# Running sums of the second attention's softplus: two reduced-precision parts instead of one full-precision operand

## What is computed

```python
z = einsum('bqkgd,bskd->bkgqs', qb, kf)              # logits
log_1m_beta = where(mask, log_sigmoid(-z), 0.0)      # minus the softplus of z, strictly causal
rev = cumsum(log_1m_beta, axis=4, reverse=True)
excl = concatenate([rev[..., 1:], zeros], axis=-1)
a = where(mask, exp(log_sigmoid(z) + excl), 0.0)
o = einsum('bkgqs,bskd->bqkgd', a, vf)
```

## The kernel before, in words

| step of | before |
|---|---|
| TensorE | sums 5, 7, 8, 12; values 8, 10, 12, 14 |
| ScalarE | shares 3, 5, 6, 10; logarithm 4, 6, 6, 10; weights 7, 9, 9, 13; out_high 9, 10, 13, 15 |
| VectorE | masked 2, 4, 6, 10; softplus 4, 6, 7, 10; less 6, 7, 8, 12; out_low 8, 10, 13, 15 |

## Time and profile before

### The profile page before, as it was taken

How to read it: one execution, slowest core, us unless ns; L and a number is a source line. 1 busy time by engine, 2 the same in 40 slices (tenths; PEclk the granted TensorE clock), 3 DMA queues, 4 the chain that set the end, 5 groups by cost and what they waited for, 6 DMA issues and landing times.

```text
span 2041.1 us, 30539 instructions
## 1 busy us (share of the span) xinstructions
PE 1908.4 (93%) x12761; PEld 1485.7 (73%) x12761; DVE 1136.2 (56%) x1523; ACT 903.7 (44%) x1289; POOL 113.3 (6%) x99
## 2 busy tenths in 40 slices
PE   9999999999999866766799999999999999999998
PEld 7898988889983211111178888888888888988887
DVE  3788877678542110101156666756666766766666
ACT  4655555554342100000045556545446555676544
POOL 0333331001000000000000000000000000000000
PEclk9999999999999977887899999999999999999999
DMA  9645447778799999999985755555555555525552
GB/s 349 214 149 170 160 158 230 233 260 288 281 367 415 425 427 425 425 426 424 421 292 196 242 189 183 171 165 170 191 191 171 186 187 188 178 93 176 186 186 83
DMA packets 241777, 503.51 MB, mean 247 GB/s; under 512 B 11473, under 2 KB 165730, under 8 KB 222434
## 3 DMA queue, kind: packets, MB, share of 16 engines
q1 hardware_dynamic: 241024, 500.96, 68.2%
q10 hardware_dynamic: 610, 0.53, 0.1%
HBM read 500.07 MB, written 1.07 MB: 246 GB/s over the span
## 4 chain that ended last, share of the span: by engine, by line
PE 80%; DMA 12%; DVE 4%; issue 2%; ACT 2%; SPq 1%; POOL 0%; DVEq 0%; ACTq 0%
PE bank L651 15%; PE bank L653 15%; PE bank L652 15%; PE bank L712 14%; PE bank L714 7%; DMA m<-in_expert_w_down 4%; DMA m<-in_expert_w_up 4%; PE bank L1115 3%; DMA m<-in_expert_w_gate 3%; PE bank L1126 2%; PE bank L996 1%; DVE m L2314 1%; SPq L3430 1%; PE bank L1390 1%; PE bank L810 0%
## 5 line engine op out<-in xcount | busy, mean ns | idle before, releaser
L2314 DVE TENSOR_TENSOR m<-m,m 128x1024 fp32r<-128x1024 f32 x505 | 626.7, 1255 | 282.7 <-ACT m L1599 281.5
L651 PE MATMUL bank<-m,m 128*128 128x256 f32 (+1 forms) x1960 | 657.9, 336 | 2.7 <-DVE m L2314 1.1
L653 PE MATMUL bank<-m,m 128*128 128x256 f32 (+1 forms) x1960 | 645.6, 329 | 0.0
L652 PE MATMUL bank<-m,m 128*128 128x256 f32 (+1 forms) x1960 | 645.3, 329 | 0.0
L1599 ACT ACTIVATE m<-m 128x1024 fp32r<-128x1024 f32 x505 | 524.7, 1054 | 212.2 <-PE bank L653 196.5
L712 PE MATMUL bank<-m,m 128*128 128x512 f32 x1248 | 439.8, 394 | 0.0
L651 PEld LDWEIGHTS bank<-m,m 128*128 128x128 f32 x1960 | 368.5, 188 | 49.8 <-issue 9.2
L653 PEld LDWEIGHTS bank<-m,m 128*128 128x128 f32 x1960 | 368.5, 188 | 36.7
L652 PEld LDWEIGHTS bank<-m,m 128*128 128x128 f32 x1960 | 368.8, 188 | 34.1 <-issue 1.2
L714 PE MATMUL bank<-m,m 128*128 128x256 f32 x1248 | 352.7, 283 | 0.0
L712 PEld LDWEIGHTS bank<-m,m 128*128 128x128 f32 x1248 | 234.4, 188 | 54.0
(11 more groups left out here) (353 smaller groups left out, 1377.9 us busy)
## 6 DMA issues: line engine op xcount, KB each, us to landing
m<-in_ffn_w_in SPq DMA_DIRECT2D x88, 1024.0 KB, 5.1
m<-in_w_in SPq DMA_DIRECT2D x60, 1024.0 KB, 5.2
m<-in_ffn_w_out SPq DMA_DIRECT2D x44, 1024.0 KB, 4.9
m<-in_expert_w_up SPq DMA_DIRECT2D x40, 1024.0 KB, 20.9
m<-in_expert_w_down SPq DMA_DIRECT2D x34, 1024.0 KB, 17.1
m<-in_expert_w_gate SPq DMA_DIRECT2D x33, 1024.0 KB, 22.9
m<-in_expert_w_gate SPq DMA_DIRECT2D x15, 2048.0 KB, 23.5
m<-in_expert_w_down SPq DMA_DIRECT2D x13, 2048.0 KB, 17.8
```

The costliest lines, as they stand in the source:

```text
L651: e.matmul(o, s[0], m[0], start=first, stop=False, skip_group_check=skip)
L652: e.matmul(o, s[0], m[1], start=False, stop=False, skip_group_check=skip)
L653: return e.matmul(o, s[1], m[0], start=False, stop=last, skip_group_check=skip)
L2314: inc(e.tensor_tensor(rv(fit(q.L, q.view.shape)), q.view, fit(q.H, q.view.shape), ALU.subtract), "l", skey(q, "L"))
```

## The change

The softplus of each group is split once more: GpSimd copies each half of t_ into fp32r at the place of l_ (the high part), and VectorE subtracts it from t_ in place (the low part). `sums` then makes, for each of three banks, two matmuls of 512 columns with SLI and two with ONES that cover 128 columns (banks 0 and 2) or two separate tiles of 128 (bank 1), all in fp32r. SLI and ONES are stored as fp32r. The steps are placed anew:

| step of | after |
|---|---|
| TensorE | sums 6, 8, 11, 13 (at 13 behind values(2)); values 8, 10, 13, 14 |
| ScalarE | shares 3, 5, 6, 10; logarithm 4, 6, 9, 10; weights 7, 8, 12, 14; out_high 9, 10, 13, 15 |
| VectorE | masked 2, 4, 6, 10; softplus 4, 6, 10, 12; low_part 5, 6, 10, 12; less 6, 8, 12, 13; out_low 9, 10, 13, 15 |

```diff
                 def sums(j, first):
                     b = [take(first + i, "sc", j, i) for i in range(3)]
-                    sp = sbuf[j][1]
-                    for n in range(12):
-                        w.wait_ge("ssp", j, n // 6)
-                        o = b[n // 4][:, 128 * (n % 4):128 * (n % 4) + 128]
-                        ins = e.matmul(o, SLI, sp[:, 128 * n:128 * n + 128], start=True, stop=n % 3 != 1, skip_group_check=True)
-                        if n % 3 == 1:
-                            ins = e.matmul(o, K(C_ONE), sp[:, 128 * n + 128:128 * n + 256], start=False, stop=True,
-                                           skip_group_check=True)
-                        if n % 4 == 3:
-                            full(ins, "sc", j, n // 4)
+                    H, L = spHL[j]
+                    for i in range(3):
+                        o = slice(512 * i, 512 * i + 512)
+                        w.wait_ge("spL", j, (512 * i + 511) // 768)
+                        e.matmul(b[i][:, :], SLI, H[:, o], start=True, stop=False, skip_group_check=True)
+                        e.matmul(b[i][:, :], SLI, L[:, o], start=False, stop=False, skip_group_check=True)
+                        if i == 1:
+                            w.wait_ge("spL", j, 1)
+                            out = b[1][:, :].rearrange("p (g n) -> p g n", n=128)[:, 0:4:3]
+                            m = [z.rearrange("p (g n) -> p g n", n=128)[:, 5:9:3] for z in (H, L)]
+                        else:
+                            c = 128 if i == 0 else 256
+                            out = b[i][:, c:c + 128]
+                            m = [z[:, 512 * i + c + 128:512 * i + c + 256] for z in (H, L)]
+                        e.matmul(out, ONES, m[0], start=False, stop=False, skip_group_check=True)
+                        full(e.matmul(out, ONES, m[1], start=False, stop=True, skip_group_check=True), "sc", j, i)
...
                 for step in range(15):
-                    if step in (5, 7, 8, 12):
-                        j = (5, 7, 8, 12).index(step)
-                        sums(j, 4 if j > 1 else 0)
-                    if step in (8, 10, 12, 14):
-                        values(step // 2 - 4)
+                    if step in (6, 8, 11):
+                        j = (6, 8, 11).index(step)
+                        sums(j, 4 if j else 0)
+                    if step in (8, 10, 13, 14):
+                        values((8, 10, 13, 14).index(step))
+                    if step == 13:
+                        sums(3, 4)
...
+                def low_part(j):
+                    l_, t_, z_ = sbuf[j]
+                    for q in range(2):
+                        o = slice(768 * q, 768 * q + 768)
+                        w.wait_ge("spH", j, q)
+                        H, L = spHL[j]
+                        inc(e.tensor_tensor(L[:, o], t_[:, o], H.bitcast(F32)[:, o], ALU.subtract), "sb", ("spL", j, q))
...
+            e.tensor_copy(ONES, K(C_ONE))
...
+            for j in range(4):
+                l_, t_, z_ = sbuf[j]
+                for q in range(2):
+                    o = slice(768 * q, 768 * q + 768)
+                    w.wait_ge("ssp", j, q)
+                    inc(e.tensor_copy(spHL[j][0][:, o], t_[:, o]), "att", ("spH", j, q))
```

More of the change, by code:

```diff
@@ L558, in build @@
         kk_of = [[kk[64 * i:64 * i + 64].rearrange("p (b h n) -> p h b n", b=2, h=2)[:, h] for h in range(2)] for i in range(2)]
-        gone, SLI = mem(20736, 768), mem(22016, 128)
+        gone, SLI, ONES = mem(20736, 768), rv(mem(22016, 128)), rv(mem(55232, 128))
         osT = hl(39456, 41504, 2048)
@@ L562, in build @@
         sbuf = [[mem(o, 1536) for o in so_[3 * j:3 * j + 3]] for j in range(4)]
+        spHL = [[rv(mem(o, 1536)) for o in so_[3 * j:3 * j + 2]] for j in range(4)]
         z_at = [0]
@@ L2044, in stick @@
                         shares(2)
-                        logarithm(2)
                     if step == 7:
                         weights(0)
+                    if step == 8:
+                        weights(1)
                     if step == 9:
                         out_high(0)
-                        weights(1)
-                        weights(2)
+                        logarithm(2)
                     if step == 10:
@@ L2056, in stick @@
                         logarithm(3)
+                    if step == 12:
+                        weights(2)
                     if step == 13:
                         out_high(2)
+                    if step == 14:
                         weights(3)
@@ L3028, in stick @@
                         masked((2, 4, 6, 10).index(step))
[L3029 to L3032, removed]
+                    if step == 4:
+                        softplus(0)
+                    if step == 5:
+                        low_part(0)
+                    if step == 6:
+                        softplus(1)
+                        low_part(1)
+                        less(0)
                     if step == 8:
-                        less(2)
+                        less(1)
+                    if step == 9:
                         out_low(0)
                     if step == 10:
+                        softplus(2)
                         out_low(1)
+                        low_part(2)
+                    if step == 12:
+                        less(2)
                         softplus(3)
-                    if step == 12:
+                        low_part(3)
+                    if step == 13:
+                        out_low(2)
                         less(3)
-                    if step in (13, 15):
-                        out_low(step // 2 - 4)
+                    if step == 15:
+                        out_low(3)
                     yield
```

## The result

The changed kernel takes 2046.7 us, median of 16 runs (2045.79 to 2049.74), against 2043.32 for 16 runs of the kernel before (2042.34 to 2045.49): ratio 1.0018, 95% interval 1.0011 to 1.0025. That is 3.4 us slower; the forecast was 2048.0 with a range of 2043 to 2055. The profiled execution was 2049.39 us with a span of 2047.6.

A forecast was written before the change was run, and what follows sets the result against it. TensorE's own work was taken as the bound. Minus 5.6 (sums) and 1.6 (old waits), plus about 9.9 (new waits) and 2.0 (clock) gave about 4.7 us slower: 2048.0 us median, range 2043 to 2055.

The forecast's parts named there:

- saved in the sums: TensorE's sums: a group falls from 3.5 to 2.1 us, saving 5.6 us in all (bounds 6.5 and 3.8).
- old waits gone: TensorE's two earlier waits for sums, 1.2 and 0.4 us, disappear: 1.6 us saved.
- first wait, logits(2): TensorE, half a piece into piece 6, idles 1.0 us before logits(2) for q2's evacuation.
- second wait, piece 10: TensorE idles 5.0 us before piece 10, which needs group 0's output, out_low(0); the largest term.
- third wait, values(2): TensorE idles 3.1 us before values(2), until ScalarE has made weights(2).
- net of all but the clock: Through the end of values(3), the new order costs 2.7 us net, sums' saving included.
- clock, first fall: After the wait before piece 10, TensorE's granted clock falls and costs 1.7 us.
- clock, second fall: After the wait before values(2), a fall adds 0.3 us, mostly hidden since sums(3) waits for VectorE anyway.
- copy, low_part: Added work: a GpSimd copy of 768 columns into fp32r takes 1.3 us, a VectorE subtraction 0.95 us.
- Waits without a fall: Rival: TensorE's new waits come but its clock stays up; plus 2.7, 2046.0 us; chance 0.20.
- TensorE stays the only bound: Rival: weights(0) to out_low(0) takes under 6 us, so piece 10 does not wait; 2037.1 us; chance 0.10.
- GpSimd's copies: Rival: copies bound the softplus-to-less line of groups 1 and 3, from about 1.8 us each; 2052 to 2058; chance 0.20.

The follow-up runs named there:

- e7: Changed kernel plus 16 idle f32 matmuls of 128 columns on TensorE before the first bo piece: 2045.06 us (before 2043.84).
- e5: The changed kernel measured again, its steps written out singly, as base for four further runs: 2048.32 us (before 2043.84).
- e4: The step order of e3, but with the f32 sums of the kernel before: 2043.23 us (before 2043.52).
- e3: Changed kernel's fp32r format in another step order, with out_high(0) ahead of weights(1) and less(0) ahead of softplus(1): 2037.81 us (before 2043.52).
- e1: Changed kernel's step order with the f32 sums of the kernel before, no split or GpSimd copies: 2045.51 us (before 2043.52).
- e8: Changed kernel with each GpSimd copy done twice: 2054.45 us (before 2043.84).
- e6: Changed kernel with ScalarE's weights(1) moved from step 8 to step 9, behind out_high(0): 2044.17 us (before 2043.84).
- e9: Changed kernel without VectorE's low_part; sums multiply the high part twice and wait for the copies alone: 2047.1 us (before 2043.84).

## Why the prediction was right, and where it was off

The sign, the mechanism and the places were right, and the total was 4.7 against 4.16 us in the stage (3.4 by medians of 16 runs). The single waits missed by 0.5 to 1.0 us and the total by only 0.5: where TensorE comes later to a gate, the wait is shorter and the gate stays where it is. By its own steps:

| step | forecast | measured |
|---|---|---|
| saved in the sums | 5.6 (1.4 a group) | 6.1 (1.5 a group) |
| old waits gone | 1.6 | 1.6 |
| first wait, logits(2) | 1.0 | 1.46 |
| second wait, piece 10 | 5.0 | 4.05 |
| third wait, values(2) | 3.1 | 2.15 |
| waits at values(0), sums(2) | 0.4, 0.2 | 0, 0 |
| waits at sums(3), piece 14, values(3) | 0.6, 0.5, 0.6 | 1.0, 0.2, 0.2 (e7); 0, 0, 0.19 (changed) |
| net of all but the clock | +2.7 | +2.0 (e7 against before) |
| clock, first fall | 1.7 | 2.1 (e5 against e7) |
| clock, second fall | 0.3 | 0 |
| copy, low_part | 1.3, 0.95 | 1.28, 1.1 |

- *The sums* were forecast from the 0.11 us row of the first attention; the pair of 128 columns takes 0.17, so one is 0.085. The range for it, half to double, held this. One group was read for all four: in e4 they take 3.5 to 3.6 us and in e3 2.0 to 2.1, 5.9 us less in all, and another 0.2 lie around them.
- *The first wait* was 0.5 too short in the forecast, because the walk took L of that piece at 1.2 us. It ran beside the first copies and took 1.85, so q2's evacuation came at 1790.33. In e1, with no copies, the wait is 0.83.
- *The second wait* was the term mis-sized most: out_low(0) ended 0.4 us earlier than walked and TensorE came 0.5 later, the other side of the first wait. In the walk's own time (minus 2.37) TensorE started piece 10 at 1810.6 against 1811.0. The chain of ten links was right to 0.4 us; the wait, a difference of two walks, was off by twice that.
- *The third wait*: in the walk's time, and without the 2.1 us of the clock, values(2) started at 1830.4 (1834.92 less 4.5) against 1831.1, and TensorE came to it at 1828.3 instead of 1828.0. Again two small errors of opposite sign add up in the wait.
- *The clock.* By the earlier trace rows 1.7 us was read from the expert stage, where TensorE at half speed worked for part of 5 us. Here 2.1 were lost: the clock was 0.50 from about 1811.0 to 1817.9, twice as long as in the expert stage of the kernel before (910.4 to 913.8), and for the first 1.9 us of it TensorE still waited. The second fall came, against my doubt, and cost nothing on balance, as I had argued: from values(2) to piece 14 the changed kernel takes 5.20 us at the low clock (1834.92 to 1840.12), and e7 takes 5.19 at full clock (1829.53 to 1834.72), since it waits 1.0 us for low_part(3) and 0.2 for out_low(2) instead. The Trainium skill, "TensorE: Matmul & The Clock Gate", section "HAM oscillation", says that an idle gap halves the clock; both falls of the changed kernel agree; the gaps of 1.46 us and e7's gap of 2.15 us had none.
- *The rivals.* "Waits without a fall" is e7: 2045.06, forecast 2046.0. "TensorE stays the only bound" was forecast at 2037.1 and is what e3 reaches at 2037.81, with another order. Its condition, a line from weights(0) to out_low(0) under 6 us, was wrong: the line takes 9.5 us there, and less(1) still stands ahead of out_low(0). What the third order did was to move weights(1) behind out_high(0) and to begin the line 4.7 us earlier. "GpSimd's copies" shows as waits for low_part before the sums at twice their price (e8); from which price on was not measured.

The balance of the stage: -6.1 for the sums, -1.6 for the old waits, +7.85 for the new ones, +2.2 for the first fall (7.2 against 5.0 us for piece 10 with logits(3)), +1.6 for the second (5.20 us from values(2) to piece 14 against 3.63 in e3; it takes the place of e7's waits at sums(3) and piece 14): 3.95 of the measured 4.16. The remaining 0.2 no row names.

## What to carry to other kernels

A saving on the bounding engine counts only up to the next gate, the place where it needs another engine's result. Before the saving is built, walk the line of the other engines to that gate, link by link. What the saving has above the slack turns into a wait. Here there was no slack (e1 already waited), and of 2.8 us saved in two groups 2.6 were waited. A wait of 4 us of TensorE cost 2.1 us of its clock on top. Then put first in each queue what TensorE waits for next, here group 0's output ahead of group 1's weights and less(0) ahead of softplus(1). And measure a change of format and a change of order in four kernels (neither, each alone, both), not in two.

## What was not expected of the hardware

- **The same wait, with and without a fall of the clock.** Before values(2) TensorE idled 2.15 us in the changed kernel, 2.14 in e6 and 2.15 in e7. The granted clock went to half in the first two and stayed at 1.00 in e7. The waits of 1.46 us were not followed by a fall, those of 4 us were; between them e8 has a wait of 2.73 us with no fall, and falls at waits of 1.79 and 1.90 us (each with one of 0.72 us a few us before or behind it), so the length of a single wait doesn't settle it. The pieces ahead of this wait are the same in all three; e6 had waited 1.47 and 0.46 us in the 25 us before it, e7 0.52. What tells them apart stays open. In e9 the first fall begins about 1811, over 1 us after TensorE had resumed at 1809.80, so a fall doesn't need to begin inside the wait.
- **GpSimd and VectorE slow each other.** In e8 a copy takes 0.83 us by itself and 1.5 us where it begins beside the second half of softplus, a VectorE instruction with two operands in SBUF (the on-chip memory of the engines), which itself keeps its length. VectorE can pay too, as its timeline in the changed kernel shows beside the first copies:

```profile
1787.84 3.25 POOL L3446 CAST m<-m 128x768 fp32r<-128x768 f32 x2 [1210.65 <-DVE m L3021]
1796.70 2.27 POOL L3446 CAST m<-m 128x768 fp32r<-128x768 f32 x2 [5.62 <-DVE m L3021]
```
```profile
1786.82 1.82 DVE L3021 SCALAR_TENSOR_TENSOR m<-m,m 128x768 f32<-128x768 f32 x2
1788.55 1.85 DVE L2326 TENSOR_TENSOR m<-m,m 128x1024 fp32r<-128x1024 f32 x1
```

The pair that meets L (L2326) takes 3.25 us instead of 2.27, and L takes 1.85 instead of 1.23. The forecast of 1.3 us for a copy came out right for a wrong reason: I scaled a plain copy by the price of the format, 0.78 to 1.3, while by itself a copy into fp32r costs 0.83, hardly more than the 0.78, and the rest is this contention. The Trainium skill, "SBUF — State Buffer", section "SBUF: two separate sides", has the port pair that the two hold exclusively; the 0.6 to 0.7 us lost on either side agree with it.
